# Turned queries of the second latent-attention half: copied out of PSUM by ScalarE instead of VectorE

## The reference, cut to what matters

```python
q = (_rms(q_lat, w['g_q_lat']) @ w['w_uq']).reshape(b, s, H_A, QK_NOPE + QK_ROPE)
q_nope = _rms(q[..., :QK_NOPE], w['g_mla_qn'])
q_rope = _rope(_rms(q[..., QK_NOPE:], w['g_mla_qr']), pos)
...
sc = (jnp.einsum('bqhd,bkhd->bhqk', qn, k_nope)
      + jnp.einsum('bqhr,bkr->bhqk', qr, kr_all)).astype(jnp.float32) * MLA_SCALE
sc = jnp.where(_chunk_mask(qp, k_pos), sc, -jnp.inf)
pr = jax.nn.softmax(sc, axis=-1).astype(v_a.dtype)
return jnp.einsum('bhqk,bkhd->bqhd', pr, v_a)
```

## Time and profile before

| | us |
|---|---|
| median of 3 runs | 996.79 |
| the three runs | 996.12, 996.79, 996.95 |
| profiled execution | 994.83 |
| its span in the trace | 993.0 |
| what lies around the span | 1.83 |
| busy in the span: PE, DVE, ACT, POOL | 897.7, 469.7, 359.1, 203.1 |

### The profile page before, as it was taken

The page is one execution under the profiler, slowest core; times in us unless marked ns, Lnnn a source line. Parts: engine busy times, 40 slices in busy tenths (PEclk is TensorE's granted clock), DMA queues, the critical chain, the costliest instruction groups (busy, mean ns, idle before and its releaser), DMA issues.

```text
span 993.0 us, 12918 instructions
## 1 busy us (share of the span) xinstructions
PE 897.7 (90%) x4489; PEld 612.9 (62%) x4489; DVE 469.7 (47%) x1130; ACT 359.1 (36%) x840; POOL 203.1 (20%) x305
## 2 busy tenths in 40 slices
PE   6899999999999899899879999989997777778998
PEld 5787878787887666645556777863332222223786
DVE  3464373737465589838787534351111111105562
ACT  3633443434243389843446422201111111114321
POOL 1332130504040144485500000010111011100100
PEclk9999999999999999999999998899999999999999
DMA  7334242422221511001413087869999999994511
GB/s 224 104 111 135 84 122 75 128 80 74 72 78 43 185 33 36 25 2 64 159 33 94 14 248 305 306 210 352 418 417 419 417 419 417 417 417 188 191 43 53
DMA packets 80085, 179.09 MB, mean 180 GB/s; under 512 B 16850, under 2 KB 32260, under 8 KB 80020
## 3 DMA queue, kind: packets, MB, share of 16 engines
q1 hardware_dynamic: 71556, 160.27, 44.9%
q0 software_dynamic: 7424, 17.98, 4.9%
q10 hardware_dynamic: 1040, 0.00, 0.1%
HBM read 163.92 MB, written 21.64 MB: 187 GB/s over the span
## 4 chain that ended last, share of the span: by engine, by line
PE 30%; DMA 17%; DVE 6%; issue 2%; ACT 1%; SPq 1%; DVEq 0%; ACTq 0%; POOLq 0%
DMA raw_e<-in_w_ei 14%; PE acc L665 5%; PE acc L793 5%; PE acc L1435 4%; PE acc L1398 3%; PE acc L681 2%; PE acc L1547 2%; DMA raw_e<-in_w_eo 2%; PE tp L1381 2%; PE acc L763 1%; PE acc L1508 1%; DMA raw<-in_w_out 1%; PE acc L1610 1%; PE tp L1531 1%; PE tp L654 1%
## 5 line engine op out<-in xcount | busy, mean ns | idle before, releaser
L1398 PE MATMUL acc<-whi,lhi 128*128 128x512 f32 (+2 forms) x432 | 169.2, 392 | 6.1 <-DVE wlo L1862 6.0
L1398 PE MATMUL acc<-wlo,lhi 128*128 128x512 f32 (+2 forms) x432 | 166.0, 384 | 0.0
L1398 PE MATMUL acc<-whi,llo 128*128 128x512 f32 (+2 forms) x432 | 165.9, 384 | 0.0
L665 PE MATMUL acc<-raw_e,xT 128*64 128x512 f32 x512 | 121.9, 609 | 32.5 <-DMA raw_e<-in_w_ei 31.0
L665 PEld LDWEIGHTS acc<-raw_e,xT 128*64 128x64 f32 x512 | 37.3, 139 | 113.4 <-issue 111.3
L1653 ACT ACTIVATE whi<-raw,gcol 128x512 fp32r<-128x512 f32 (+2 forms) x96 | 61.5, 689 | 121.6 <-issue 115.2
L1398 PEld LDWEIGHTS acc<-whi,lhi 128*128 128x128 f32 x432 | 81.5, 189 | 25.1 <-DVE wlo L1862 9.1
L1398 PEld LDWEIGHTS acc<-whi,llo 128*128 128x128 f32 x432 | 81.5, 189 | 16.7
L1398 PEld LDWEIGHTS acc<-wlo,lhi 128*128 128x128 f32 x432 | 81.6, 189 | 15.5
L1862 DVE SCALAR_TENSOR_TENSOR wlo<-raw,gcol,whi 128x512 fp32r<-128x512 f32 (+2 forms) x96 | 64.8, 716 | 47.7 <-ACT whi L1653 47.6
L1083 DVE TENSOR_TENSOR gg<-acc,gg 128x256 f32<-128x256 f32 x16 | 6.8, 425 | 138.2 <-ACT gg L816 138.2
(11 more groups left out here) (267 smaller groups left out, 1492.0 us busy)
## 6 DMA issues: line engine op xcount, KB each, us to landing
raw_e<-in_w_ei SPq DMA_DIRECT2D x128, 512.0 KB, 16.0
raw_e<-in_w_eo SPq DMA_DIRECT2D x64, 512.0 KB, 16.4
raw<-in_w_in SPq DMA_DIRECT2D x40, 512.0 KB, 3.7
raw<-in_w_out SPq DMA_DIRECT2D x8, 512.0 KB, 6.6
wp_raw<-in_w_ple_gate SPq DMA_DIRECT2D x8, 512.0 KB, 7.6
raw_e<-y_rows SPq DMA_DIRECT2D x4, 1024.0 KB, 8.5
va_rows<-raw POOLq DMA_DIRECT2D x12, 256.0 KB, 3.1
vh<-va_rows SPq DMA_DIRECT2D x8, 384.0 KB, 3.6
```

Source lines behind the costliest of these rows:

```text
L665: mm = pe.matmul(acc[rows, 0, :], xT[:, 2 * c + k, rows], raw_e[:, slots[2 * c + b], 512 * k:512 * k + 512], start=(c == 0 and k == 0), st ...
L1398: mm = pe.matmul(bank, x, W[w], start=(kk == 0 and x is hi and w == 0), stop=(kk == c.kt - 1 and x is lo))
```

## The change

The copy of the second half's turned queries leaves VectorE's loop (it was one step behind the transposes) and goes into ScalarE's, into the step of the transposes, between copy_turned(n-4) and exps(n). It is an `activation` with `Copy` on 96 partitions of up to 4 x 128 elements. Since `t_copied` counts copies in one engine's order, the five copies get a semaphore of their own, `uq_copied`, and the keys of `last_uq` are taken out of the numbering. Nothing else changes: the transposes, their banks and the values are the same.

```diff
+        uq_copied = sem("uq_copied")
...
-        copied = number([k for k in tgroups if k[0] not in ("attn_b", "attn_a", "hn")])
+        copied = number([k for k in tgroups if k[0] not in ("attn_b", "attn_a", "hn", last_uq)])
...
             if key in copied:
                 eng.wait_ge(t_copied, copied[key] + 1)
+            elif key[0] == last_uq:
+                eng.wait_ge(uq_copied, key[1] + 1)
...
                     if ph == "a" and n == n_units // 2:
-                        pe.wait_ge(t_copied, copied[(last_uq, TILES - 1, 0)] + 1)
+                        pe.wait_ge(uq_copied, TILES)
...
                     if lag <= n < n_units + lag:
                         copy_turned(n - lag)
+                    if ph == "a" and n in TURN_AT:
+                        t, hs = TURN_AT[n], slice(H // 2, H)
+                        act.wait_ge(t_done, tg[(last_uq, t, 0)] + 1)
+                        act.activation(qT[0:HD, hs, t * P:t * P + ROWS[t]],
+                                       tp[0:HD, tg[(last_uq, t, 0)] % 2, :].rearrange("p (k r) -> p k r", r=P)[:, :, 0:ROWS[t]],
+                                       ACT.Copy).then_inc(uq_copied, 1)
...
                 if n in NORM_AT:
                     normalise(last_uq, [NORM_AT[n]])
-                if n - 1 in TURN_AT:
-                    copy_turned(last_uq, [TURN_AT[n - 1]])
```

## The result

| | before | after |
|---|---|---|
| median, us | 996.79 | 989.37 |
| lowest to highest (5 runs each) | 992.62 to 997.33 | 987.88 to 992.36 |
| profiled execution, us | 994.83 | 990.63 |
| its span, us | 993.0 | 988.8 |

The ratio is 0.993 with a 95% interval of 0.9911 to 0.9949: faster by 5.1 to 8.9 us. Measured again twice beside the kernel before, the changed kernel had medians of 990.56 against 997.0 (0.9933, 0.9917 to 0.9949) and 991.61 against 997.1 (0.9935, 0.9913 to 0.9957).

What follows compares the result with a forecast made beforehand. First half of attention "a": PE and DVE wait in turn; second half: PE-bound. Leads 0.54 + 2.03 - 0.82 + 1.13 + 1.47 + 1.03 = 5.38, up to 5.95 with overlap, taken as 5.7: 996.79 - 5.7 = 991.1 us; range 989.6 to 994.4.

Steps and rivals of the forecast that it cites:

- PE's five waits: PE's waits for DVE's copy into qT in steps 8, 11, 14, 17 and 20 go, 6.20 us in all.
- Four were to cost nothing: ACT's copies before exps(6), (9), (12), (15) fit its idle stretches of 1.85, 2.27, 1.59 and 1.71 us; cost 0.
- The fifth, without cover: ACT's last copy, before exps(18), has no idle stretch; exps(18) would be some 0.4 us late, total cost taken as 0.
- The rule of the Trainium skill: Plain arithmetic belongs on VectorE: an ACT copy would take 2.04 us, hold step 18 by 0.5 to 1.0, giving 991.6 to 992.1.
- Steps 14 and 17: Probabilities' copies on ACT come in time, the first by 0.58 us; no new wait, PE's lead grows by 1.13 and 1.47.
- Step 11's new wait: values(6) waits for unit 6's probabilities behind exps(9), maxima(9) and normalise(2): 0.82 of the 2.57 us lead is lost, leaving 1.75.
- the overlap that printed idle times leave out: Without a wait PE's next start precedes the modelled end, 0.06 to 0.17 us at each of five places, 0.6 in all.
- step 8: PE's wait of 0.54 us goes; values(3), gate_out(3), normalise(2) and maxima(9) come 0.54 earlier.
- step 20: PE's wait of 1.03 us before scores(20) goes, bringing the lead to 5.38 us.
- B: Rival: first half of the attention stays bound by DVE, only the copies' 2.7 us gained, 994.1 us; chance 0.20.
- C: Rival: no change, the lead is lost behind the attention in the stages streaming expert weights, 996.8 us; chance 0.08.
- D: Rival: slower, ACT's queue becomes the bound and each copy delays exps, 999.5 us if at all five; chance 0.06.

Runs made afterwards that it cites:

- e2: Kernel before, copies still on DVE but moved in front of maxima(n); 992.46 us, scores(0) to scores(20) 34.81 us against 39.19 before.
- e6: Changed kernel with two extra 128x256 products on DVE at each of the five steps where its copies stood; 990.75 us, scores(0) to scores(20) 34.31 us.
- e3: Changed kernel with each of ACT's five copies made twice; 989.61 us, scores(10) to scores(20) 17.15 us, as in the changed kernel.
- e4: Changed kernel with the five copies left out, so heads 4 to 7 use old values; 991.24 us, scores(10) to scores(20) 17.15 us.
- e5: Changed kernel with DVE's normalisation of a query tile moved from the end of step n to behind maxima(n+1); 987.26 us, scores(0) to scores(20) 32.53 us.
- a0: The changed kernel measured again, unchanged, beside the kernel before; 990.56 us against 997.0, scores(0) to scores(20) 33.18 us.
- e7: e5 with the normalisations of tiles 0 and 1 moved later still; 989.43 us, scores(0) to scores(20) 32.74 us.

## Why the prediction was right, point by point

**The forecast.** 991.1 was forecast and 989.37 measured; in the two repetitions 990.56 and 991.61. The first median lies 0.2 below the low end of the range, 989.6, the other two inside it. Direction and cause came out as forecast; my range took too little account of how whole times move: the three differences to the kernel before beside it are 7.4, 6.4 and 5.5 around the stage's 6.0, so that the distance of 989.37 from 991.1 is mostly chance. It allowed for the three runs shown (996.12 to 996.95), while more runs of the kernel before reached from 991.91 to 1001.81.

**What the change removes.** PE's five waits are gone and no L1886 is left in attention "a" (in the changed kernel that line is L1895, and its last copy, of the first half's queries, starts at 483.0). DVE's queue is shorter by its 2.7 us; e2 and e6 say how to weigh the two. Position alone gets 4.38, and putting 4.4 us of work back costs 1.14 up to scores(20) and 1.76 in all. The relief of DVE is a smaller part, but it is not nothing.

**What it adds.** ACT's copies: 0.59 forecast and 0.59 measured, the short one 0.39 and 0.38. Four were to cost nothing because of the idle stretches before exps; these shrank from 1.85, 2.27, 1.59 and 1.71 to 1.01, 1.52, 1.05 and 1.32, and e3 and e4 showed no cost in the stretch from 10 to 20. The fifth, without cover, was taken at 0 as well, and the same two runs bear that out. The rule of the Trainium skill (ScalarE: Activation LUTs, Rules for kernel authors) that I had weighed against the change gives its factor of up to about 3 for bf16, and did not carry over to fp32 here: a copy of 2.04 us is nowhere, the row says 0.59. I had also called 2.04 under or close to the four idle stretches; it is over three of them (1.85, 1.59 and 1.71), so that case could have cost more than the 0.5 to 1.0 that I gave it.

**The sum, wait by wait.** Steps 14 and 17 were covered, as worked out: unit 9's probabilities were ready 0.38 us before values(9) began (508.12 - 507.74; 0.58 forecast), unit 12's 0.64 before values(12) (513.14 - 512.50). Step 11's new wait was forecast as 0.82 before values(6), behind exps(9) and the normalisation, and is printed as 0.81; e5 confirmed the chain by moving the normalisation. The term that I mis-sized is the overlap that printed idle times leave out. I put it at 0.6, took half of it, 5.7 between 5.38 and 5.95, and the stage gave 6.02. By starts in the two timelines, the lead grew by 0.73 in step 8, 2.10 in step 11, 1.30 in step 14, 1.63 in step 17 and 1.16 in step 20, 6.92 in all where 6.20 were printed, so all of the overlap counts and it is 0.7; and the new wait took back 0.90 by starts, not 0.82. values(6), 20.92 us behind scores(0) before (503.15 - 482.23), is now 18.99 behind (502.75 - 483.76): a lead of 1.93, not 1.75.

**What carries it to the end.** From scores(20) to the load behind the attention 51.49 us before and 51.36 to 51.39 after: nothing is given back there. The profiled executions differ by only 4.2, not 6.0, because scores(0) began 1.53 us later in the changed one, ahead of anything that was changed, and because another 0.4 went behind the load (572.91 - 568.29 = 4.62 at the load). Early on its clock was lower, as this row of each shows, first before, then after:

```profile
20.00:40.00 20.00, 17.32 (x100) 16.31 (x98) 4.21 (x12) 11.73 (x23) 3.73 (x10) 1.00 0.52 162
```

```profile
20.00:40.00 20.00, 18.02 (x95) 17.50 (x94) 4.38 (x12) 11.25 (x22) 3.71 (x10) 0.91 0.50 159
```

Whether that alone made the 1.53 I did not test: a0 has 1.00 there and began 0.84 late. The start of scores(0) moves without any edit: it is at 483.03, 483.07 and 483.76 in three executions of the changed kernel, and at 482.60 and 484.04 in two of e5. That the two kernels with DVE's copies have the earliest of all twelve (482.23 and 482.06 in e2) is not explained; with one execution each it proves no cost of the change ahead of the stage and excludes none. The absolute forecasts (scores(20) at 515.7, span 987.3) miss by this shift: 516.93 - 1.53 = 515.40.

**The rivals.** B (2.7 us, DVE stays the bound) is refuted by the missing waits at steps 14 and 17 and by e6. Against B I had also set 7.9 us in which DVE waited for values; that is the sum over the whole attention, and only 4.0 of it lie in the first half, before scores(20). C (given back later) is refuted up to the load. The stages behind it, from that load to the read of the experts' rows, take 345.91 us before, 346.15 to 346.86 in the three executions of the changed kernel, and 343.18 to 347.42 in the edits, in no order that follows them; so a loss of up to 1 us there could not be seen, and isn't excluded. D (ACT's queue on the path) is refuted by e3.

## What to carry to other kernels

When two PSUM banks are shared by streams whose copies are made by different engines, ask of each copy not how long it takes but what stands before it in its engine's queue: here a copy of 0.7 us held PE for up to 2 us, and moving it past four small operations on the same engine brought 4.4 of 6.0 us. When a wait is taken away, look at the very next instruction and at what stands before its own source: that is where the next wait is, and its size can be worked out from the old trace. And measure a change of half a per cent by the stretch between two starts in the trace, which repeats to 0.01 us here when the clock is the same, rather than by whole times, which spread over 8 to 10 us in a dozen or more runs.

## What was not expected of the hardware

PE's granted clock fell to 0.50 for some 3.4 us in two of eleven profiled executions of kernels that keep the same idle 1.83 us shortly before (e7, which has no such idle, left out), and cost 1.6 us each time; the others kept 1.00 there. In e3 it fell before the first instruction that the edit touches. An edit that leaves work out can so look slower by 1.6 us (e4) for reasons that aren't the edit's. What decides whether it falls, no run here shows.
